# RWKV-7 scan of a two-layer encoder trunk: how the old state joins the new one, and the order of the products in a chunk step

## What is computed

```python
def wkv7_scan(r, w, k, v, kk, a, reverse):
    def step(state, inp):
        r_t, w_t, k_t, v_t, kk_t, a_t = inp
        sa = jnp.einsum('bhvk,bhk->bhv', state, -kk_t)
        state = (state * w_t[:, :, None, :]
                 + sa[..., None] * (kk_t * a_t)[:, :, None, :]
                 + v_t[..., None] * k_t[:, :, None, :])
        y = jnp.einsum('bhvk,bhk->bhv', state, r_t)
        return state, y
    ...
    _, ys = lax.scan(step, state0, xs, reverse=reverse)
```

## Time and profile before

| | us |
|---|---|
| median of 3 runs | 1809.8 (1809.66 to 1811.24) |
| the profiled execution | 1816.97 |
| its span | 1815.0 |
| PE busy / DVE busy / ACT busy in it | 1625.1 / 1013.9 / 737.1 |
| mean granted clock of PE | 0.948 |
| scan rounds of layer 0 / layer 1 | 309.7 to 475 / 1198 to 1361 |

### The profile page before, as it was taken

How to read it: one execution, slowest core, us unless ns; L and a number is a source line. 1 busy time by engine, 2 the same in 40 slices (tenths; PEclk the granted TensorE clock), 3 DMA queues, 4 the chain that set the end, 5 groups by cost and what they waited for, 6 DMA issues and landing times.

```text
span 1815.0 us, 29245 instructions
## 1 busy us (share of the span) xinstructions
PE 1625.1 (90%) x11880; PEld 1189.7 (66%) x11880; DVE 1013.9 (56%) x1533; ACT 737.1 (41%) x1203; POOL 289.7 (16%) x124
## 2 busy tenths in 40 slices
PE   2899877888989999989989988598889899999997
PEld 0776434656768888877757744266667688887885
DVE  6664669886336767754334243778841544445233
ACT  3443254665543322222234343457653333323222
POOL 1333000000122222212304310000003122222121
PEclk8899987999999999999989999699999999999999
DMA  7354210000225555533303310000003222222221
GB/s 302 115 183 163 84 47 1 3 2 2 77 87 185 186 185 185 185 128 131 137 23 119 93 55 1 1 3 3 3 2 116 70 93 92 92 92 92 93 92 70
DMA packets 34659, 163.08 MB, mean 90 GB/s; under 512 B 3841, under 2 KB 4097, under 8 KB 25857
## 3 DMA queue, kind: packets, MB, share of 16 engines
q1 hardware_dynamic: 34560, 161.65, 25.5%
HBM read 159.54 MB, written 2.10 MB: 89 GB/s over the span
## 4 chain that ended last, share of the span: by engine, by line
PE 55%; issue 28%; DVE 8%; ACT 4%; POOL 4%; DMA 0%; POOLq 0%; DVEq 0%; ACTq 0%
PE bank L505 8%; PE bank L507 7%; PE bank L506 7%; PE bank_pair L505 3%; PE bank_pair L507 3%; PE bank_pair L506 3%; POOL work_parts L1932 2%; PE bank L552 2%; PE bank L852 2%; PE bank L853 2%; POOL proj_weights_parts L1927 2%; PE bank_pair L609 1%; PE bank L830 1%; PE bank L666 1%; PE bank L868 1%
## 5 line engine op out<-in xcount | busy, mean ns | idle before, releaser
L505 PE MATMUL bank<-work_parts,y_mix_parts 128*128 128x512 f32 x792 | 316.1, 399 | 20.6 <-DVE work_parts L1698 10.3
L507 PE MATMUL bank<-work_parts 128*128 128x512 f32 x792 | 315.5, 398 | 0.0
L1711 DVE TENSOR_TENSOR work_parts<-work,y_mix_parts 128x1024 fp32r<-128x1024 f32 x66 | 169.6, 2569 | 257.8 <-ACT y_mix_parts L982 257.8
L1927 POOL TENSOR_TENSOR proj_weights_parts<-proj_weights,proj_weights_hi_parts 128x1024 fp32r<-128x1024 f32 x54 | 130.4, 2422 | 884.5 <-ACT proj_weights_hi_parts L978 796.0
L1932 POOL TENSOR_TENSOR work_parts<-work,y_mix_parts 128x1024 fp32r<-128x1024 f32 x66 | 159.1, 2410 | 608.5 <-ACT y_mix_parts L982 608.5
L982 ACT ACTIVATE y_mix_parts<-work 128x1024 fp32r<-128x1024 f32 x132 | 133.0, 1054 | 263.3 <-DMA work<-mlp_dram 253.6
L506 PE MATMUL bank<-work_parts,y_mix_parts 128*128 128x512 f32 x528 | 209.0, 396 | 0.0
L505 PEld LDWEIGHTS bank<-work_parts,y_mix_parts 128*128 128x128 f32 x792 | 150.6, 190 | 58.3 <-issue 24.0
L507 PEld LDWEIGHTS bank<-work_parts 128*128 128x128 f32 x792 | 150.4, 190 | 35.9
L505 PE MATMUL bank<-work_parts,proj_weights_hi_parts 128*128 128x512 f32 x272 | 112.5, 413 | 26.6 <-DVE work_parts L1698 24.4
L506 PEld LDWEIGHTS bank<-work_parts,y_mix_parts 128*128 128x128 f32 x528 | 100.5, 190 | 24.4
(11 more groups left out here) (279 smaller groups left out, 2991.0 us busy)
## 6 DMA issues: line engine op xcount, KB each, us to landing
work<-mlp_dram SPq DMA_DIRECT2D x66, 1024.0 KB, 4.9
work<-ada_dram SPq DMA_DIRECT2D x64, 512.0 KB, 4.7
proj_weights<-tiles_dram SPq DMA_DIRECT2D x57, 512.0 KB, 3.6
x_res<-ada_dram SPq DMA_DIRECT2D x24, 512.0 KB, 4.6
x_res<-x_dram SPq DMA_DIRECT2D x2, 2048.0 KB, 10.7
mixer_inputs<-ada_dram SPq DMA_DIRECT2D x8, 512.0 KB, 17.6
work<-mlaw_dram SPq DMA_DIRECT2D x4, 640.0 KB, 5.2
out_dram<-x_res SPq DMA_DIRECT2D x8, 256.0 KB, 2.2
```

The lines of the kernel that those rows point to most:

```text
L505: mm(out, w_hi, x_hi, start=start, stop=False)
L507: return mm(out, w_lo, x_hi, start=False, stop=stop)
L1711: TTT(MW_L[q][:, 1], MW_IN[q][:, 1], plain(MW_H[q][:, 1]), ALU.subtract).then_inc(msp_v.sem, msp_v.one("l1"))
L1927: pool.tensor_tensor(ring_l[s], ring[s], plain(ring_h[s]), ALU.subtract).then_inc(spl_q.sem, spl_q.one(f"t{s}"))
```

## The change

The old state is no longer copied by PE. DVE adds it: for s > 0, `scan_state` on DVE is now an addition (bank 1 plus the old state, into the new one), a wait for its own end, and the multiplication with the decay in place. The product with the identity is gone, so the solve opens bank 1 in every step. On PE, in steps 1 to 5, one direction of the Gram blocks stands ahead of the solve and the other behind it; the token transposes stand ahead of the update; in all steps from 1 the values stand behind the output. Step 0 keeps its order.

```diff
         sc_p = steps("sc_p", ["G0", "K0", "G1", "L0", "K1"] + [n for s in range(NCH) for n in ([f"R{s}"] if s else []) + [f"SA{s}"]
-                     + ([f"G{s + 2}"] if s < NCH - 2 else []) + (["S0", "L1"] if s == 0 else [f"L{s + 1}", f"S{s}"] if s < NCH - 1 else [])
-                     + ([f"K{s + 2}"] if s < NCH - 2 else [])] + ["Y"])
+                     + ([f"G{s + 2}"] if s < NCH - 2 else []) + ([f"K{s + 2}"] if 0 < s < NCH - 2 else []) + ([f"S{s}"] if s < NCH - 1 else [])
+                     + ([f"L{s + 1}"] if s < NCH - 1 else []) + (["K2"] if s == 0 else [])] + ["Y"])
...
-        sc_v = steps("sc_v", ["G0", "G1"] + [n for s in range(NCH - 1) for n in [f"S{s}"] + ([f"G{s + 2}"] if s < NCH - 2 else [])])
+        sc_v = steps("sc_v", ["G0", "G1"] + [n for s in range(NCH - 1) for n in ([f"A{s}"] if s else []) + [f"S{s}"] + ([f"G{s + 2}"] if s < NCH - 2 else [])])
...
-            def scan_gram(it, s):
+            def scan_gram(it, s, sides=(0, 1)):
 
                 p = it % 2
-                if s:
-                    pe.wait_ge(sc_v.sem, sc_v.at(f"G{s - 1}", it))
-                else:
-                    pe.wait_ge(sc_v.sem, sc_v.before(f"G{NCH - 1}", it))
-                    pe.wait_ge(pre_v.sem, pre_v.at("k1", it))
-                for d in D2:
+                if sides[0] == 0:
+                    if s:
+                        pe.wait_ge(sc_v.sem, sc_v.at(f"G{s - 1}", it))
+                    else:
+                        pe.wait_ge(sc_v.sem, sc_v.before(f"G{NCH - 1}", it))
+                        pe.wait_ge(pre_v.sem, pre_v.at("k1", it))
+                for d in sides:
...
-                own(sc_p, last, f"G{s}")
+                if sides[-1] == 1:
+                    own(sc_p, last, f"G{s}")
...
-                if s < NCH - 1:
-                    for e in range(2):
-                        rows = slice(64 * e, 64 * e + 64)
-                        mm(PS[1][rows, 2 * P:3 * P], ident[rows, 64 * e:64 * e + 64], cur[rows].rearrange("p d v -> p (d v)"), start=True,
-                           stop=False, skip_group_check=True)
...
-                    last = mm(corner(PS[1], d, e), XT[it % 2][rows, d, s, :], RHS[rows, d, :], start=(s in (0, NCH - 1) and d == 0), stop=True,
+                    last = mm(corner(PS[1], d, e), XT[it % 2][rows, d, s, :], RHS[rows, d, :], start=(d == 0), stop=True,
...
+                        if 0 < s < NCH - 2:
+                            scan_gram(it, s + 2, (0,))
                         scan_solve(it, s)
                         if s < NCH - 2:
-                            scan_gram(it, s + 2)
-                        if 0 < s < NCH - 1:
-                            scan_values(it, s + 1)
+                            scan_gram(it, s + 2, (1,) if s else (0, 1))
+                        if 0 < s < NCH - 2:
+                            scan_tokens(it, cur, s + 2)
                         last = scan_update(it, s)
                         if s == 0 and build:
                             rwkv_triangle(new, 1)
+                        if s < NCH - 1:
+                            scan_values(it, s + 1)
                         if s == 0:
-                            scan_values(it, 1)
-                        if s < NCH - 2:
-                            scan_tokens(it, cur, s + 2)
+                            scan_tokens(it, cur, 2)
...
                 dve.wait_ge(sc_p.sem, sc_p.at(f"S{s}", it))
-                own(sc_v, TTT(SM[(s + 1) % 2], PS[1][:, 2 * P:3 * P].rearrange("p (d v) -> p d v", d=2),
-                              EM[it % 2][:, :, s].unsqueeze(2).to_broadcast([P, 2, C]), ALU.mult), f"S{s}")
+                grown, state = PS[1][:, 2 * P:3 * P].rearrange("p (d v) -> p d v", d=2), SM[(s + 1) % 2]
+                if s:
+                    own(sc_v, TTT(state, grown, SM[s % 2], ALU.add), f"A{s}")
+                    dve.wait_ge(sc_v.sem, sc_v.at(f"A{s}", it))
+                    grown = state
+                own(sc_v, TTT(state, grown, EM[it % 2][:, :, s].unsqueeze(2).to_broadcast([P, 2, C]), ALU.mult), f"S{s}")
```

## The result

| | before | after |
|---|---|---|
| median, us | 1810.52 (4 runs, 1809.66 to 1812.14) | 1822.84 (4 runs, 1819.82 to 1824.69) |
| ratio | | 1.0065, 95% interval 1.0048 to 1.0083 |
| profiled execution: time / span / clock | 1816.97 / 1815.0 / 0.948 | 1822.65 / 1820.7 / 0.951 |
| PE / DVE / ACT busy in it | 1625.1 / 1013.9 / 737.1 | 1613.1 / 1022.1 / 737.2 |

The changed kernel is slower by 12.3 us (0.65%). The forecast had the sign as its second likeliest case and was too low: 1813.3, range 1808.5 to 1817. PE has 12.0 us less to do, DVE 8.2 us more, and the kernel lost time: neither engine's total sets the end here, the loop between them does.

What follows compares the result with a forecast made beforehand. The prediction saw a scan step bounded by the PE-ACT-DVE loop and PE's own work, almost equally long. Update delay (+0.07), addition (+0.33) and helper-step relief (-0.26) summed to +1.76 per layer, +3.5 us: 1809.8 to 1813.3, range 1808.5 to 1817.

Steps and rivals of the forecast that it cites:

- Plain step: Full scan step without helpers: 3.17 us by the loop against 3.13 before, +0.04.
- Step 6: Scan step with nothing else to do: 3.10 us against 2.77 before, +0.33.
- The addition: Second, dependent DVE operation for the state: state ready 0.33 us later, bounds 0.20 and 0.40.
- The step with L521: Step 4 of rounds 0 and 1, decay products waiting behind both new delays: 5.43 us, +0.40.
- Round 0 as a whole: Steps 1 to 6 of round 0 in each layer: +1.23 us together.
- Rival 1: Transposes hold up the update, some 27 steps pay 0.18 more: 1818 us; chance 0.20 together with the clock going wrong.
- Rival 2: Second DVE operation costs 0.20 us instead of 0.33: 1809.8 to 1810.5, no change; chance 0.16.
- Rival 4: PE's relief outweighs DVE's delay everywhere, full step under 2.93 us; chance 0.09 together with the clock's fast side.
- A step that ends on a 512-column helper: Steps ending on L545, L695 or L700: update to helper 0.78 us instead of 1.11, so -0.26 a step.
- Steps 1 and 2 of rounds 1 to 3 together: First two scan steps of these rounds, ACT setting the time from 1 to 2: -0.28 us in round 1.
- Step 1 of round 0: First scan step of round 0, counted like a step without helpers: +0.04 us.
- rival 3: PE's clock at round ends: 1805 us if fast (0.09 with PE's relief), 1817 if wrong (0.20 with transposes in the way).

Runs made afterwards that it cites:

- f3: Changed kernel without the addition, the old state left out and the new order of PE kept: 1808.0 us, ratio 0.9979 to the kernel before.
- e3: Kernel before with only the new order of PE; identity product and single DVE operation stay: 1810.83 us, ratio 0.9999.
- f4: Changed kernel, old state times decay ahead of DVE's wait for PE, then two independent 64-column operations: 1820.93 us, ratio 1.0050 to the kernel before.
- e2: Kernel before with the identity product out and the DVE addition in, PE's order as before: 1821.53 us, ratio 1.0046.
- g4: Kernel before without the identity product and without an addition, in the old order: 1813.62 us, ratio 1.0004.
- h1: Changed kernel once more, nothing altered, one profiled execution: 1820.37 us.
- h2: Kernel before once more, nothing altered, one profiled execution: 1811.89 us.
- f1: Changed kernel plus unused 512-column products on PE between rounds (3 in rounds 0 and 1, 5 in round 2): 1823.06 us, ratio 1.0063 to the kernel before.
- f2: Kernel before plus unused 512-column products on PE between rounds (3 in rounds 0 and 1, 5 in round 2): 1813.25 us, ratio 1.0010.
- g1: Changed kernel plus fewer unused 512-column products between rounds (1 in round 0, 2 in rounds 1 and 2): 1816.47 us, ratio 1.0027 to the kernel before.
- g2: Kernel before plus fewer unused 512-column products between rounds (1 in round 0, 2 in rounds 1 and 2): 1807.19 us, ratio 0.9964.
- h4: Kernel before plus unused 512-column products between rounds (1 in round 0, 2 in rounds 1 and 2), measured again: 1806.16 us, ratio 0.9977.

## Why the prediction was wrong

**Right, step by step.** Plain step 3.17 forecast, 3.19 measured, in f3 without the addition 2.86 (forecast less its 0.33: 2.84). Step 6 3.10 and 3.10. The addition 0.33 and 0.32. L673 at 2.00 and 2.02. The step with L521 5.43 and 5.46. Round 0 as a whole +1.23, measured from 21.14 to 22.35 in layer 0 (in layer 1, of which below, to 22.53). Round 2's steps 4 to 6 +1.06 and +1.06. The addition on the path in 28 places makes 9.2 us; f3 and the changed kernel are 9.5 apart (8.8 to 9.6 without the long first steps, so the nearness is in part luck). Rival 1, the transposes in the way, is refuted: L673 stands 2.02 into the step, and e3's and f3's plain steps are shorter than before, not longer. Rival 2, a cheap second operation, is refuted by f3; it is half true only for operations that don't wait for each other (f4). Rival 4 is refuted too: without any price for the old state (f3) PE's relief is worth 2.6 us.

**The term that failed: what PE's relief gives back.** It is the two terms below. The sum of +3.5 stood on 9.2 us of addition less 5.7 of relief. Measured were 9.5 less 2.6 to 2.8.
- *A step that ends on a 512-column helper, -0.26*: measured -0.07 (3.99 to 3.92), and -0.07 for L700's step in round 3 too. The working took 0.78 from the update to the helper and let the next step follow as before, 0.95 later. The rows have 0.85 (369.70 to 370.55) and 1.06 (370.55 to 371.61). In the kernel before the helper followed the transposes, which have its own shape (128*128), and its record began 0.11 behind the last of them while this was still running; so the 0.95 was no full duration. This is the neighbour in the kernel before, 0.11 ahead of L545's 371.61:

```profile
371.50 0.27 PE L625 MATMUL bank<-constants,work 128*128 128x128 f32 x1
```

  Behind the values (128*64) it starts 0.33 after them. From its start to the next state product it is 0.95 in both kernels of the old order (before, e2) and 1.05 or 1.06 in all three of the new one (e3, f3, after): a distance between starts was used for a group whose neighbour had changed. That the change of shape is the reason is argued, not shown. e3 has 3.99 in this step, because with the copy in it the update stands 2.09 into the step and not 2.01, and e2 has 3.99 too: the 0.07 needs the new order and the copy gone.
- *Steps 1 and 2 of rounds 1 to 3 together, -0.28*: measured -0.08 (9.38 to 9.30). The table shows that two things are mixed here: the new order costs 0.14 to 0.15 (e3 against before, f3 against g4), and taking the copy away gives 0.22 (g4 against before), which the prediction had put at nothing, since PE waited for ACT at that place. In step 1 it doesn't: there the centring product L690 stands between state and solve, and PE is the later one. From ACT's right-hand side in step 2 to the start of step 3 it is 3.50 before (365.07 to 368.57) and 3.43 in the changed kernel (to 367.69), which is the 0.07 of the other helper steps once more:

```profile
364.26 0.28 ACT L1114 ACTIVATE rstd<-bank 128x128 f32<-128x128 f32 x1
```

These two terms stand at three places each in a layer and were off by 0.19 and 0.20 us: 1.2 per layer, 2.4 in all. With them the sum is +5.9. The terms listed for round 1 add to +0.19 and not +0.16, which matters little.

A smaller term was left out:

- *Step 1 of round 0*, put at +0.04 like every plain step: 3.39 against 3.13 in layer 1, in all four executions (layer 0 has it in one). There DVE is behind, which the working had only for step 3: a transposition of 1.97 us and a copy end just ahead of the addition, which starts 2.72 into the step and not 2.52. This adds some 0.2 us. From h1, layer 1:

```profile
1199.71 0.45 PE L649 MATMUL bank<-rstd,work 64*64 64x64 f32 x8
...
1200.11 1.97 DVE L1517 STREAM_TRANSPOSE work<-work 64x1024 f32<-64x1024 f32 x1 [1.62 <-ACT work L1063]
...
1202.11 0.29 DVE L1522 COPY work<-work 64x256 f32<-64x256 f32 x1
1202.43 0.29 DVE L1614 TENSOR_TENSOR rstd<-bank,rstd 128x128 f32<-128x128 f32 x1
```

The executions have +6.1 (h1 against h2) to +6.9; the spread is the first step of a round, which takes 4.26 or, partly at the lower clock, 4.46 to 5.17 in round 3.

**From 6 to 7 us in the steps to 10 in the time.** The 12 runs of the changed kernel have a mean of 1822.0 (standard error 0.9), the 110 of the kernel before, over all sets, 1811.7 (0.4): +10.3. The profiled executions alone have a mean span of 1818.4 (four) and 1811.5 (three): +6.9, as the steps. The other runs of the changed kernel went slower at a lower clock: the mean granted clock is 0.9494 over its 12 runs and 0.9514 before. Over the 110 runs of the kernel before, a straight line gives 1.5 us for each 0.001 of mean clock, so this lower clock is worth some 2.9 us, an estimate. Done with the means of f1 and f2 the same sum leaves 5.8 of 9.6 us (their steps differ by 5.6), with g1 and g2 7.4 of 9.6 (6.2). That is rival 3 in the wrong direction, and it comes on top of the steps. Where in the kernel the unprofiled runs lost it, their records don't say; the four profiled ones lost 15.3 to 17.6 us of full speed between the rounds against 12.7 to 14.0, which points there, but they are few, and the stretches were longer than before in two of four only (133.4 and 134.2 us). This part is argued, not shown.

**The starting point.** The 1809.8 of three runs was low: the kernel before came to 1810.3 to 1812.5 in its later sets. About 2 of the 9.5 us by which the forecast was low are this, 2.4 the helper steps and steps 1 and 2, 0.2 step 1 of round 0, about 3 the clock, if the estimate holds; the rest lies within the spread. The range was too narrow for another reason as well: it held the clock going wrong and the relief failing as alternatives, and they came together.

## What to carry to other kernels

Before moving work to an engine that is mostly idle, look at which steps its operations are on the path: 8 us more of DVE work cost 9.5 us of steps although DVE stood at 56%, because each of them lay in the loop. Gains from a new order and costs of a longer loop must not be added: a shorter PE part uncovers the loop, so that the same addition cost 6 to 7 us in the old order and 9 to 9.5 in the new one. A distance between starts may be carried over only if the neighbours, too, have the same shape as before.

## What the runs showed of the hardware

- **A second DVE operation of 128 columns that needs the first costs 0.32 us; one operation split into two independent halves costs 0.18.** Single 128x128 operation: 0.35 us to the next state product (f3); two dependent ones 0.67 (after); two of 64 columns without dependence 0.53 (f4).
- **SBUF was no cheaper than PSUM here.** L1617 reads SBUF alone and took 0.29, L1614 and the old L1613, which read PSUM, 0.29 too. The table in the Trainium skill (VectorE: DVE Perf Modes, the TRN2 errata section) would make the first 0.19; the same section adds that the measured fixed part is about 150 cycles, which gives 0.29 as an estimate. The trace agrees with this sentence and not with the table.
- **Change of shape.** With the old state left out in both, the step with L545 went from 4.00 (g4) to 3.92 (f3) only, although the new order takes 0.27 from a plain step (3.13 to 2.86). The Trainium skill (TensorEngine Tiling (Array Packing), Key Properties) says that PE drains at such a change, without a price; the rows here have the helper 0.33 behind the start of eight 128x64 products (L634 to L545), where the next group of the same shape comes after 0.28 (L673 to L679).
- **Products without a use can pay.** One or two products of 512 columns in gaps of 1.65 to 2.8 us between rounds made the kernel before 0.2 to 0.4% faster (g2 and h4), the fastest kernel of this case; three in the smallest gap, and five in the last, took the gain back (f2; ratio 1.0010).
